# A second pair of scores placed in the middle of the unit that leads each attention

## What is computed

```python
for layer in range(DEPTH):
    x = x + mixers[layer](rms_norm(x, mix_norms[layer]))      # even_mixer, odd_mixer
    x = x + memory_cross_attention(rms_norm(x, xn), rms_norm(mem, mn), wq, wkv, wo)
    x = x + swiglu(rms_norm(x, fn), wg, wu, wd)
```

```python
s = jnp.einsum('bqhd,bkhd->bhqk', q, k) * scale      # plus mask, bias or sink
p = jax.nn.softmax(s, axis=-1)
o = jnp.einsum('bhqk,bkhd->bqhd', p, v)
```

## Time and profile before

| what | value |
|---|---|
| median of the runs | 2003.89 us (2003.71 to 2009.75, 3 runs) |
| the profiled execution's own time | 2004.48 us |
| its span, first to last instruction | 2002.6 us |
| PE busy | 1940.7 us, 97% |
| VectorE (DVE) busy | 1261.5 us, 63% |
| ScalarE (ACT) busy | 885.9 us, 44% |
| GpSimd (POOL) busy | 167.0 us, 8% |
| moved by DMA | 317.56 MB, mean 159 GB/s |
| granted TensorE clock, each of 40 slices | 9 tenths or more |

### The profile page before, as it was taken

How to read it: one execution, slowest core, us unless ns; L and a number is a source line. 1 busy time by engine, 2 the same in 40 slices (tenths; PEclk the granted TensorE clock), 3 DMA queues, 4 the chain that set the end, 5 groups by cost and what they waited for, 6 DMA issues and landing times.

```text
span 2002.6 us, 33109 instructions
## 1 busy us (share of the span) xinstructions
PE 1940.7 (97%) x13572; PEld 1703.3 (85%) x13572; DVE 1261.5 (63%) x2184; ACT 885.9 (44%) x1508; POOL 167.0 (8%) x187
## 2 busy tenths in 40 slices
PE   7999999999999999999999999999999999999998
PEld 7769999998689999978688887888888998997887
DVE  6765666677556666544434447667677745677776
ACT  5655543445565444424532334322232536455443
POOL 0220000002103100002511000000000012000000
PEclk9999999999999999999999999999999999999999
DMA  7365699955646565323533333454656422664554
GB/s 239 102 214 165 157 234 220 220 171 165 224 145 189 182 214 161 116 77 125 163 96 100 95 106 110 133 179 155 197 180 198 139 85 62 186 195 140 182 183 137
DMA packets 313325, 317.56 MB, mean 159 GB/s; under 512 B 17079, under 2 KB 291398, under 8 KB 312918
## 3 DMA queue, kind: packets, MB, share of 16 engines
q1 hardware_dynamic: 308156, 301.65, 49.6%
q0 software_dynamic: 3904, 12.03, 3.0%
q10 hardware_dynamic: 1114, 1.76, 0.3%
HBM read 306.54 MB, written 8.85 MB: 157 GB/s over the span
## 4 chain that ended last, share of the span: by engine, by line
PE 86%; DVE 7%; ACT 3%; DMA 2%; issue 1%; POOL 0%; SPq 0%; DVEq 0%; ACTq 0%; POOLq 0%
PE acc L696 20%; PE acc L697 19%; PE acc L698 19%; PE acc L746 8%; PE acc L745 4%; DVE w_low L2024 3%; PE pss L921 2%; PE acc L742 1%; PE acc L711 1%; ACT w_high L1473 1%; PE pst L933 1%; PE acc L712 1%; PE acc L713 1%; DMA raw<-in_w_mod 1%; PE acc L948 1%
## 5 line engine op out<-in xcount | busy, mean ns | idle before, releaser
L2024 DVE TENSOR_TENSOR w_low<-raw,w_high 128x1024 fp32r<-128x1024 f32 (+4 forms) x503 | 561.1, 1156 | 140.5 <-ACT w_high L1473 137.3
L1473 ACT ACTIVATE w_high<-raw 128x1024 fp32r<-128x1024 f32 (+4 forms) x503 | 471.7, 984 | 375.6 <-PE acc L698 234.2
L696 PE MATMUL acc<-normed,w_high 128*128 128x256 f32 (+1 forms) x1768 | 565.6, 320 | 0.7 <-DVE w_low L2024 0.6
L698 PE MATMUL acc<-normed,w_low 128*128 128x256 f32 (+1 forms) x1768 | 560.6, 317 | 0.0
L697 PE MATMUL acc<-normed,w_high 128*128 128x256 f32 (+1 forms) x1768 | 560.6, 317 | 0.0
L696 PEld LDWEIGHTS acc<-normed,w_high 128*128 128x128 f32 x1768 | 336.1, 190 | 27.0 <-issue 2.0
L698 PEld LDWEIGHTS acc<-normed,w_low 128*128 128x128 f32 x1768 | 336.2, 190 | 22.5
L697 PEld LDWEIGHTS acc<-normed,w_high 128*128 128x128 f32 x1768 | 336.3, 190 | 22.0
L746 PE MATMUL acc<-inner,w_high 128*128 128x512 f32 x612 | 218.2, 396 | 0.0
L696 PE MATMUL acc<-inner,w_high 128*128 128x512 f32 (+2 forms) x576 | 197.3, 343 | 2.2 <-DVE w_low L2024 2.0
L697 PE MATMUL acc<-inner,w_high 128*128 128x512 f32 (+2 forms) x576 | 196.0, 340 | 0.0
(11 more groups left out here) (281 smaller groups left out, 2685.9 us busy)
## 6 DMA issues: line engine op xcount, KB each, us to landing
raw<-in_w_ff SPq DMA_DIRECT2D x128, 512.0 KB, 4.2
raw<-in_w_mod SPq DMA_DIRECT2D x96, 512.0 KB, 4.4
raw<-in_w_in SPq DMA_DIRECT2D x84, 512.0 KB, 4.1
raw<-in_l_w_gate SPq DMA_DIRECT2D x44, 512.0 KB, 5.5
raw<-in_l_w_up SPq DMA_DIRECT2D x44, 512.0 KB, 4.5
raw<-in_l_w_down SPq DMA_DIRECT2D x32, 512.0 KB, 4.5
raw<-in_l_w_qkv SPq DMA_DIRECT2D x24, 512.0 KB, 4.6
raw<-in_l_w_out SPq DMA_DIRECT2D x16, 512.0 KB, 4.4
```

What stands on the lines that cost most here:

```text
L696: mm(dst, lh, rh, start=i == 0, stop=False)
L698: ins = mm(dst, ll, rh, start=False, stop=i == n - 1)
L1473: nc.scalar.activation(WH[:, s % NSPLIT, w0:w0 + nw], RAW[:, r:r + nw], ACT.Copy).then_inc(w_high, 1)
L2024: V.tensor_tensor(WL[:, s % NSPLIT, c], RAW[:, r:r + nw], WH[:, s % NSPLIT, c].bitcast(F32), ALU.subtract).then_inc(w_low, 1)
```

## The change

In the four attentions named, the lead is cut in two and the scores of pair 1 stand between the halves on TensorE: in the first attention between the keys and the rotations, in the dilated one between the two token blocks (`values_in_two()`), in the neighbourhoods between the two banks (`values_in_two([0, 1], [2, 3])`). On VectorE `maxima(1)` comes right after `inverse(1)`, ahead of the lead's ropes and of the split. On ScalarE `exps(2)` and `exps(3)` come after the first half's copies and ahead of the second half's (in the dilated attention ahead of the only copy), and so ahead of the split. GpSimd's and SyncE's orders stay. Cross attentions stay as they were (`early=False`). The diff:

```diff
--- before.py
+++ after.py
@@ -798,6 +798,33 @@
                              ready if i == 0 else None)
                     used()
 
+            def values_in_two(*blocks):
+
+                held = []
+
+                def token_block(t):
+                    if not held:
+                        held.append(grid(take(KD, 256), KD, 256))
+                        held.append(bank())
+                    (wh, wl), b = held
+                    c = slice(P * t, P * t + P)
+                    return product(b[:, 256 * t:256 * t + 256], [((at_pair.high[:, k, c], at_pair.low[:, k, c]),
+                                                                  (wh[:, k, :], wl[:, k, :])) for k in range(KD)])
+
+                def last_block():
+                    token_block(1).then_inc(acc_full, 1)
+                    used()
+
+                def first_bank():
+                    held.append(grid(take(KD, 256), KD, 256))
+                    straight(held[0], 256, at_pair, KD, blocks[0])
+
+                def last_bank():
+                    straight(held[0], 256, at_pair, KD, blocks[1])
+                    used()
+
+                return (first_bank, last_bank) if blocks else (lambda: token_block(0), last_block)
+
             def modulate(accs, cols):
 
                 u, q = st["unit"], st["freed"]
@@ -953,7 +980,12 @@
                 copied(have - 1 if keys is None else keys)
                 pe.wait_ge(rope_done, turned_by if ropes is None else ropes)
                 scores(0)
-                if lead is not None:
+                early = isinstance(lead, tuple)
+                if early:
+                    lead[0]()
+                    scores(1)
+                    lead[1]()
+                elif lead is not None:
                     lead()
                 cols, rows, spare = (PSACC[(st["acc"] + i) % 4] for i in (1, 2, 3))
                 out_banks[first] = [PSO, spare, rows, PSS[0]] if pairs == 2 else [PSO, spare]
@@ -968,7 +1000,8 @@
                             pe.wait_ge(rope_done, turned_by)
                         if j + 1 == late:
                             pe.wait_ge(rope_done, st["rope"])
-                        scores(j + 1)
+                        if j or not early:
+                            scores(j + 1)
                     if j == 1:
                         for g in range(st["acc"] - 4, st["acc"]):
                             copied(g)
@@ -1142,10 +1175,15 @@
                     used()
                     heads = lambda x, k: x[:, k, :].rearrange("p (h d) -> p h d", h=8)[:, :, 64:128]
 
-                    def mla_lead():
-                        wh, wl = w = grid(take(2, 1024), 2, 1024)
+                    latent = []
+
+                    def mla_keys():
+                        latent.extend(grid(take(2, 1024), 2, 1024))
                         need(st["store"])
-                        turned(w, [P * h for h in range(8)], ckvn, 2, S)
+                        turned(latent, [P * h for h in range(8)], ckvn, 2, S)
+
+                    def mla_values():
+                        wh, wl = latent
                         rotate(mla_raw, const("rot_mla"), "mla", st["acc"] - 5)
                         for t in range(NB):
                             c = slice(P * t, P * t + P)
@@ -1156,7 +1194,7 @@
                         used()
 
                     st["store"] += 1
-                    attention(swa_tasks + mla_tasks, MODS, lead=mla_lead, tail=heads_product, late=SWA_H // 2,
+                    attention(swa_tasks + mla_tasks, MODS, lead=(mla_keys, mla_values), tail=heads_product, late=SWA_H // 2,
                               keys=st["acc"] - 3)
                 else:
                     out = []
@@ -1173,7 +1211,7 @@
                         else:
                             rotate(dil_raw[i - 2:i - 1], const("rot64"), "dil", out[i - 2])
                     values(1)
-                    attention(dil_tasks, MODS, lead=lambda: values(1), tail=heads_product)
+                    attention(dil_tasks, MODS, lead=values_in_two(), tail=heads_product)
                 pe.wait_ge(cols_free, st["pair"])
                 side_by_side(3, ot)
                 project(1, at_pair.tokens(S, 2 * S))
@@ -1299,7 +1337,7 @@
                     gates.append(take(8, P))
                     turned(grid(gates[0], 8, P), [0], at_pair, KD, T)
 
-                attention(na_tasks(l), 0 if l else MODS, lead=lambda: values(1, blocks=[0, 1, 2, 3]), tail=gate_tail,
+                attention(na_tasks(l), 0 if l else MODS, lead=values_in_two([0, 1], [2, 3]), tail=gate_tail,
                           keys=st["acc"] - 3, ropes=st["rope"] - 1)
                 if l == 0:
                     bias_split.append(st["split"] + 1)
@@ -1625,15 +1663,21 @@
                         nc.scalar.activation(d.high[:, 0, :], out_bank(first, lots[n])[:, 0:S], ACT.Copy)\
                             .then_inc(high_done, 1)
 
+                early = isinstance(lead, tuple)
                 for j in range(pairs + 2):
                     for e in range(2):
-                        if j < pairs:
+                        if j < pairs and not (early and j == 1):
                             exps(2 * j + e)
                         if 0 < j <= pairs:
                             probs(2 * j - 2 + e)
                         if mods and e == 0:
                             modulation_rows(rows + min(max(j - 1, 0), mods) // 2)
-                    if j == 0 and lead is not None:
+                    if j == 0 and early:
+                        lead[0]()
+                        exps(2)
+                        exps(3)
+                        lead[1]()
+                    elif j == 0 and lead is not None:
                         lead()
                     for e in range(2):
                         if j > 1:
@@ -1735,15 +1779,17 @@
                     copy_out(mq[0:96, 6:8, :], lambda b: shape2(b)[0:96], 96 ** -0.5)
                     split()
 
-                    def mla_lead():
+                    def mla_keys():
                         for i in range(4):
                             copy_out(mk[0:64, 2 * i:2 * i + 2, :], lambda b: shape2(b)[0:64])
+
+                    def mla_values():
                         st["acc"] += 5
                         for i in range(NB):
                             copy_out(mv[:, i, :])
                         split()
 
-                    attention(swa_tasks + mla_tasks, MODS, lead=mla_lead)
+                    attention(swa_tasks + mla_tasks, MODS, lead=(mla_keys, mla_values))
                 else:
                     g = st["acc"]
                     st["acc"] += 1
@@ -1768,7 +1814,7 @@
 
                     for i in range(3):
                         v_lead(i)
-                    attention(dil_tasks, MODS, lead=lambda: v_lead(3))
+                    attention(dil_tasks, MODS, lead=(lambda: None, lambda: v_lead(3)))
                 residual(1)
                 split()
                 first = 2 * st["res"]
@@ -1890,14 +1936,15 @@
                     split()
                     st["acc"] += 1
 
-                def na_lead(i):
-                    for j in range(2):
-                        copy_out(v_na[:, 2 * j:2 * j + 2, S * i:S * i + S], shape2)
-                    split()
-                    st["acc"] += i == 0
-
-                na_lead(0)
-                attention(na_tasks(l), 0 if l else MODS, lead=lambda: na_lead(1))
+                def na_values(i, j):
+                    copy_out(v_na[:, 2 * j:2 * j + 2, S * i:S * i + S], shape2)
+                    if j:
+                        split()
+                        st["acc"] += i == 0
+
+                na_values(0, 0)
+                na_values(0, 1)
+                attention(na_tasks(l), 0 if l else MODS, lead=(lambda: na_values(1, 0), lambda: na_values(1, 1)))
                 for b3 in range(3):
                     for m in range(KD):
                         b, free = bank()
@@ -2333,7 +2380,7 @@
                     ins.then_inc(free, 1)
                     own(free)
 
-            def attention(tasks, mods=0, lead=None, both=False, between=()):
+            def attention(tasks, mods=0, lead=None, both=False, between=(), early=True):
                 first, pairs = st["task"], len(tasks) // 2
                 done = st["mod"]
                 lots, slots = lots_before(tasks), prob_slots(tasks)
@@ -2391,12 +2438,14 @@
                 split()
                 inverse(0)
                 inverse(1)
+                if early:
+                    maxima(1)
                 if lead is not None:
                     lead()
                 for j in range(1, pairs + 3):
                     if 1 < j <= pairs:
                         inverse(2 * j - 2)
-                    if j < pairs:
+                    if j < pairs and not (early and j == 1):
                         maxima(j)
                     if 1 < j <= pairs:
                         inverse(2 * j - 1)
@@ -2515,7 +2564,7 @@
```

(2 more changed lines are left out.)

## The result

The kernel after takes 2009.15 us (median of 22 runs, 2007.07 to 2013.09), the kernel before 2006.03 us on the same chips (median of 22 runs, 2001.94 to 2010.38). The ratio is 1.0018, 95% interval 1.0012 to 1.0025: 3.6 us slower (2.4 to 5.0). The forecast was 2004.6 in a range of 2000.5 to 2007.5: the sign was right, the size and the range were not. Part of the miss is the base. The median of before was 2003.89 over three runs and 2006.03 over 22; the other part, 3.1 to 3.6 us where +0.75 was forecast, is what the experiments are about.

What follows compares the result with a forecast made beforehand. The chain was taken as 86% TensorE, a microsecond counting only where TensorE has nothing to issue or its next dependency moves. Terms +0.9 + 0.15 + 0.15 - 0.45 = +0.75 us gave 2004.6, range 2000.5 to 2007.5.

Steps and rivals of the forecast that it cites:

- the sign: Whole kernel: the change was forecast to make it slower, by +0.75 us.
- the base: Whole kernel: median of the kernel before, taken as 2003.89 us, from which the forecast of 2004.6 was reckoned.
- The insertion and what it does to each head: All four heads: pair 1's scores inside the leading unit make its end 1.05 us later, 1.26 in the neighbourhoods, delaying the split.
- The gaps of 4.61 us: TensorE's idle time before the third pair's scores: 1.50 first attention, 0.85 dilated, 1.13 each neighbourhood; removable directly by earlier scores.
- the first rival: All four heads: DVE and ACT absorb the late split and 4.61 us of gaps vanish, 1999.3 us; chance 0.18, wholly or mostly.
- The neighbourhoods' term: Two neighbourhood heads: DVE, though free earlier, waits for ACT's later split; a loss of 0.15 us each, 0.3 together.
- The transposes at 935.66 follow through inverse and POOL; plus 0.15: First neighbourhood head: DVE begins the split at 932.95 instead of 932.80, and the transposes come 0.15 us later.
- again plus 0.15: Second neighbourhood head: same spacing as the first, DVE's split at 1660.2 instead of 1660.07; a loss of 0.15 us.
- The dilated term: Dilated head: split, third pair's minima and the transfer each come 0.9 us later, so the head loses 0.9 us.
- The first attention's term: First attention's head: minima leave DVE's chain, so split, inverse and later scores come earlier; a gain of 0.45 us.
- it stands 0.6 above the median of the runs: Whole kernel: the profiled execution of before, 2004.48 us, against the median 2003.89; used to turn 2005.2 into 2004.6.

Runs made afterwards that it cites:

- the last version above: First head early, second neighbourhood head early and reordered, dilated and first neighbourhood heads as before, against the kernel before: 0.9991 (0.9981 to 1.0002), -1.8 us.

## Why the prediction was wrong

*The insertion and what it does to each head* was right: split, third minima and transfer at the dilated head +0.91, +0.86, +0.91 for 0.9; the first attention -0.44 for -0.45; the second neighbourhood section +0.24 for 0.15 where the clock holds. The first neighbourhood's section is +0.23 in two of seven profiles and +0.45 to +0.86 in five, with no low stretch in any. The gaps of 4.61 us went from their places but as much waiting came up behind them, so the first rival did not come true. The rule of the Trainium skill that it stood on (page "Perfetto Trace Analysis", section "Optimization Strategy": find the gap on the contended engine and start its dependency sooner) is not borne out at these heads: 0.85 and 1.05 us at the dilated one became 2.14.

*The neighbourhoods' term* failed, in the step "The transposes at 935.66 follow through inverse and POOL; plus 0.15", taken over for the second head as "again plus 0.15". The prediction had no term for the clock at all. It followed the instructions and did not ask what becomes of TensorE's waits when the scores between them are gone: 1.13 and 1.00 join to 2.39, and the clock falls behind that in five of six profiles. +1.54 instead of +0.15, the largest error of a term by the sections. At the first of the two the waits are shorter, 1.01 and 0.34 where one of 1.13 was, and the section costs +0.5 on average (0.55 - 0.07), for 0.15; where the rest of that comes from is open. These waits, in the kernel after:

```profile
937.73 0.63 PE L960 MATMUL pst<-cst,scores 128*128 128x128 f32 x4 [1.01 <-ACT probs_t L1656]
...
939.70 0.66 PE L960 MATMUL pst<-cst,scores 128*128 128x128 f32 x4 [0.34 <-POOL scores L1448]
```

*The dilated term* was right as a mechanism, in that split, third minima and transfer are 0.9 late. It left out ScalarE's copy of the first pair's probabilities, which is what TensorE waits for behind the third scores. Its size is +0.8 by sections and +1.9 ± 0.5 by runs; the forecast took the distance at the head for the cost of the whole loop, whose length is set by transfers that come early or late. The microsecond between the two sizes is open.

*The first attention's term* is -0.45 at its place but 0.0 over its section and in the runs. Among the profiles without a low clock there the section is about 0.4 shorter with the head early (mean -0.09 of three against +0.28 of five). With the head early, five of eight have a low stretch in the section, without it three of eight. So it may be the clock that takes the gain back; with so few profiles neither the 0.4 nor the counts prove it.

*The base.* The step "it stands 0.6 above the median of the runs" leaned on three runs of a kernel that scatters by 8 us. That put forecast and range 2.1 us too low. Over 22 runs of before, the range would have ended at 2009.6, and 2009.15 would have been within; that would have been luck, since three of four terms were off.

By sections the sum is now 0.0 + 0.8 + 0.5 + 1.5 = +2.8 (± 0.6), by the fit +3.5; measured are +2.8 and +3.6. The totals agree within their errors; the shares of the parts, the dilated one's above all, do not agree as well.

## What to carry to other kernels

When a wait is to be removed by issuing work earlier, look at what then lies between the waits that remain: two short ones with work between can join to one long one, and the granted clock may fall behind it. Before a split or a release is pushed behind other work, follow the buffer it frees to the transfer and to its reader. And where single runs scatter by more than the effect, compare sections between landmarks over several profiles, with the clock beside each.

## What was not expected of the hardware

One idle stretch of 2.39 us in otherwise dense work was followed by half the granted clock in 5 of 6 profiles, at a price of 1.5 to 1.6 us; idle stretches of 1.13 and 1.00 us, whose ends are 2.7 us apart, were followed by it in none of 6. Yet 0.85 and 1.05 us at the dilated head were followed by it in 3 of 11.

Many low stretches come and go between executions of code that is the same in both. In the cross attention behind the first attention (202 to 210 us) the clock was at half in 13 of 20 profiles, with that head early in 9 of 12, as before in 4 of 8, and the section was 1.1 to 1.7 us longer each time. In the dilated section, which transfers pace, a low stretch cost nothing that shows while the head was early (+0.07 with, +0.10 without, three profiles each).

These stretches are a smaller part of the 8 us by which runs of one kernel differ than one would think. Over the 344 timed runs for which a clock is on record, time and mean clock, each against the mean of its own kernel on its chip, are related only loosely (correlation -0.43, 0.6 us for 0.001 of clock), which is about a fifth of the variance. The start takes up to 3.5 us more. And from 226 to 488 us, where no variant changes anything and no profile has a low clock, the length lies between 1.38 us less and 2.87 us more than in the profile of before. In the longest one (the last version above) TensorE waits 2.9 us there for VectorE's half of weight splits, where in the profile of before it waits 0.9, besides the 0.4 that both have.
